# Decoder layer step on one Trainium2 core: layer norms with shifted, compact statistics, and the last norm finished on token rows

## The reference, cut to what matters

```
x = post(x, 0.5 * swiglu(mod(x, 0), ffn1), 0)        # FFN 1
m = mixer(mod(x, 1))                                 # attention over pages, and convolution
x = post(x, m, 1)
x = post(x, 0.5 * swiglu(mod(x, 2), ffn2), 2)        # FFN 2
mod(t, i)     = t * (1 + scale_i(c)) + shift_i(c)
post(t, y, i) = layernorm(alpha * t + gate_i(c) * y, ln_g[i], ln_b[i])
layernorm(v)  = (v - mean(v)) * rsqrt(mean((v - mean(v))^2) + 1e-5) * g + b    # over 1024 features
```

## Time and profile before

| | us |
|---|---|
| median of 3 runs (lowest, highest) | 938.13 (937.85, 939.4) |
| profiled execution, its own time | 937.36 |
| its span, first to last instruction | 935.5 |

### The profile page before, as it was taken

The page is one execution under the profiler, slowest core; times in us unless marked ns, Lnnn a source line. Parts: engine busy times, 40 slices in busy tenths (PEclk is TensorE's granted clock), DMA queues, the critical chain, the costliest instruction groups (busy, mean ns, idle before and its releaser), DMA issues.

```text
span 935.5 us, 16896 instructions
## 1 busy us (share of the span) xinstructions
PE 854.9 (91%) x6712; PEld 751.9 (80%) x6712; DVE 470.2 (50%) x751; ACT 343.2 (37%) x465; POOL 267.1 (29%) x319
## 2 busy tenths in 40 slices
PE   5699999998799988999986889869889999999997
PEld 3499989997699968988764556538789999999995
DVE  1543433432233379753686776743773454453436
ACT  2323332331222255454443324363363433432223
POOL 2020000000010013999999999600220000000000
PEclk9599999999799999999999999989999999999999
DMA  9957778777677442433998999996414544634301
GB/s 305 350 191 259 231 231 258 230 232 255 206 234 244 150 142 84 152 126 119 348 319 265 365 350 374 348 347 222 134 54 138 171 135 147 195 125 158 124 1 57
DMA packets 181521, 195.87 MB, mean 209 GB/s; under 512 B 11811, under 2 KB 163609, under 8 KB 181445
## 3 DMA queue, kind: packets, MB, share of 16 engines
q1 hardware_dynamic: 174541, 188.47, 61.9%
q10 hardware_dynamic: 6624, 6.33, 2.1%
q0 software_dynamic: 288, 0.14, 0.1%
HBM read 192.09 MB, written 3.17 MB: 209 GB/s over the span
## 4 chain that ended last, share of the span: by engine, by line
PE 78%; DVE 11%; DMA 5%; ACT 3%; issue 2%; SPq 1%; ACTq 0%; DVEq 0%
PE bank L1409 19%; PE bank L1410 18%; PE bank L1411 18%; PE bank L1625 5%; PE bank L1385 3%; PE bank L1650 3%; PE bank L1720 2%; DVE wlo L973 2%; PE bank L1374 1%; PE bank L1422 1%; DVE kT L1214 1%; PE bank L1423 1%; PE bank L1424 1%; DMA raw<-in_w_ada 1%; DMA xrow<-in_x_sample 1%
## 5 line engine op out<-in xcount | busy, mean ns | idle before, releaser
L973 DVE TENSOR_TENSOR wlo<-raw,whi 128x2048 fp32r<-128x2048 f32 (+1 forms) x80 | 190.8, 2386 | 257.6 <-ACT whi L656 256.3
L1409 PE MATMUL bank<-mh,whi 128*128 128x320 f32 x824 | 261.0, 317 | 4.5 <-DVE wlo L973 4.5
L1411 PE MATMUL bank<-mh,wlo 128*128 128x320 f32 x824 | 255.5, 310 | 0.0
L1410 PE MATMUL bank<-ml,whi 128*128 128x320 f32 x824 | 255.4, 310 | 0.0
L656 ACT CAST whi<-raw 128x2048 fp32r<-128x2048 f32 (+1 forms) x80 | 148.5, 1861 | 258.6 <-PE bank L1411 171.3
L1409 PEld LDWEIGHTS bank<-mh,whi 128*128 128x128 f32 x824 | 155.7, 189 | 15.3 <-issue 10.3
L1410 PEld LDWEIGHTS bank<-ml,whi 128*128 128x128 f32 x824 | 155.9, 189 | 0.0
L1411 PEld LDWEIGHTS bank<-mh,wlo 128*128 128x128 f32 x824 | 155.5, 189 | 0.0
L1409 PE MATMUL bank<-hh,whi 128*128 128x320 f32 x352 | 109.7, 312 | 0.0
L1410 PE MATMUL bank<-hl,whi 128*128 128x320 f32 x352 | 108.6, 309 | 0.0
L1411 PE MATMUL bank<-hh,wlo 128*128 128x320 f32 x352 | 108.6, 308 | 0.0
(11 more groups left out here) (237 smaller groups left out, 1151.8 us busy)
## 6 DMA issues: line engine op xcount, KB each, us to landing
...
```

Source lines behind the costliest of these rows:

```text
L973: dve.tensor_tensor(wl(slot_w(phase, u))[:, 0:size], landed(phase, u)[:, 0:size], wh(slot_w(phase, u))[:, 0:size].bitcast(F32), ALU.subtra ...
L1409: pe.matmul(bank[:, b, 0:T], wh(slot)[:, c], h_, start=(start and n == 0), stop=False)
L1410: pe.matmul(bank[:, b, 0:T], wh(slot)[:, c], l_, start=False, stop=False)
L1411: ins = pe.matmul(bank[:, b, 0:T], wl(slot)[:, c], h_, start=False, stop=(stop and n == len(parts) - 1))
```

## The change

- **Shift.** After the first four chunks of `yT` POOL has their sum (three additions). PE multiplies it by 1/1024 (`shift`, one matmul between two products: in DN1 and DN2 after the first half of unit 7, in WOUT after that of unit 2). DVE subtracts twice that, which is the mean of these 512 features, from the four chunks it has and from the last four chunks of `xT`, to which the later results are added (four instructions of 640 columns).
- **Statistics.** ACT squares chunk by chunk as they come, POOL adds the squares and chunks 4 and 5 (`square_sum`, `late_sum`), and PE takes mean and mean square of the shifted values with 64 output partitions for each half of the tokens (`spread`: two matmuls of 160 columns each). Difference, root and reciprocal are on 160 columns; two matmuls spread the result over 128 partitions again. A one-element root ahead loads ACT's table.
- **Scaling.** DVE subtracts the rest of the mean two chunks at a time, in the loop of chunks, and multiplies from PSUM.
- **alpha** is multiplied once into gain and bias of the first two norms; `scale_x` stays only for the first sub-layer.
- **Slots.** WIN's units 0 to 8 take slots 2, 0, 1 in turn, unit 9 slot 0. `lo(WIN, 1)` stands between the last two residuals, `hi(WIN, 2)` after the root. The first two units of w_out land in `kvw`, the last value pages take `araw`.
- **WOUT.** Four products of it move ahead in the last value pages; the first two banks are finished before the other two.
- **UP2.** Its first four banks are summed together, chunk by chunk.
- **Last norm.** PE sums each token's values with the activations as weights (`token_sums`: four matmuls with one column), transposes the shifted `yT`, and DVE finishes on token rows with mean and root per partition: two instructions of 512 columns for each of five pieces. Gain and bias come by DMA on all partitions. The two instructions on `xT` chunks in `norm` under `elif q % 2` are never reached, since `norm` now runs for n < 2 alone.

```diff
-        return phase[0] + u - (2 if u < 2 else 3)
+        if u == 0:
+            return -1
+        return phase[0] + u - (2 if u == WIN[2] - 1 else 3)
...
-        return (WIN[0] + 9, WIN[0] + 7, WIN[0] + 8, WOUT[0])[u]
+        return (WIN[0] + 9, WIN[0] + 8, WIN[0] + 6, WOUT[0])[u]
...
-                for q in range(1, NCH - 1):
+                for q in range(1, 4):
...
+            def late_sum(n):
+
+                pool.wait_ge(y_ready, 8 * n + 6)
+                pool.wait_ge(shift_ready, n + 1)
+                pool.tensor_tensor(tmp[:, 3, :], yT[:, 4, :], yT[:, 5, :], ALU.add).then_inc(ysum_step, 1)
...
+            def norm(n):
+
+                y_sums(n)
+                for q in range(1, 5):
+                    square_sum(n, q)
+                late_sum(n)
+                square_sum(n, 5)
...
+            pool.tensor_scalar(par1[:, 72:88], par1[:, 72:88], ALPHA, None, ALU.mult)
+            pool.tensor_scalar(par1[:, 96:112], par1[:, 96:112], ALPHA, None, ALU.mult).then_inc(fold_ready, 1)
+            norm(0)
...
-            scale_x(1)
...
+                    act.wait_ge(yc_ready, 2 * n + q // 2 + 1)
+                else:
+                    act.wait_ge(y_ready, 8 * n + q + 1)
+                if q >= 2:
+                    act.wait_ge(sqsum_step, 5 * n + max(q - 2, 1))
+                act.activation(tmp[:, q % 2, :], yT[:, q, :], ACT.Square).then_inc(sq_ready, 1)
...
+                    if u == 7:
+                        for q in range(4):
+                            square(n, q)
+                    if u == 9:
+                        square(n, 4)
+                        square(n, 5)
...
+            def norm(n, first, meanwhile=lambda: None):
+
+                act.wait_ge(ld_con, 16)
+                act.activation(warm[:, :], con[:, C_EPS:C_EPS + 1], ACT.Sqrt)
+                for q in range(first, NCH):
+                    square(n, q)
+                act.wait_ge(rest_ready, n + 1)
+                act.activation(tmp[:, 0, 0:NSPREAD], bank[:, NORM_BANKS[n][2], 0:NSPREAD], ACT.Square).then_inc(dsq_ready, 1)
+                act.wait_ge(vd_ready, n + 1)
+                act.activation(tmp[:, 0, 0:NSPREAD], tmp[:, 0, 0:NSPREAD], ACT.Sqrt, scale=16.0 ** -2, bias=con[:, C_EPSQ:C_EPSQ + 1]).then_inc(std_ready, 1)
+                meanwhile()
...
-            hi(WIN, 2)
-            norm(0)
+            down(DN1, WIN, 0)
+            norm(0, 6, lambda: hi(WIN, 2))
...
+            for q in range(4):
+                square(1, q)
             hi(UP2, 1)
-            norm(1)
+            norm(1, 4)
...
-                    dve.wait_ge(v_used, 24 + 5 + u)
...
+                dve.wait_ge(shift_ready, n + 1)
+                for q in (0, 1):
+                    y = yT[:, 2 * q:2 * q + 2, :]
+                    dve.scalar_tensor_tensor(y, sums, -2.0, y, ALU.mult, ALU.add).then_inc(yc_ready, 1)
+                for q in (2, 3):
+                    x = xT[:, 2 * q:2 * q + 2, :]
+                    dve.scalar_tensor_tensor(x, sums, -2.0, x, ALU.mult, ALU.add).then_inc(xs_ready, 1)
+                dve.wait_ge(xs_ready, 2 * n + 2)
...
+                    if u == 7:
+                        shift(sub)
...
+                            if nxt is not None and last and cc == 0:
+                                lo(nxt, u + SLOTS - phase[2])
...
+                dve.wait_ge(var_ready, n + 1)
+                dve.wait_ge(dsq_ready, n + 1)
+                dve.tensor_tensor(small[0], bank[:, NORM_BANKS[n][3], 0:NSPREAD], small[0], ALU.subtract).then_inc(vd_ready, 1)
+                dve.wait_ge(std_ready, n + 1)
+                dve.reciprocal(small[1], small[0]).then_inc(nr_ready, 1)
...
+                centre(0)
+                dve.wait_ge(spread_mm, 2 * n + 2)
...
+                    if q in (2, 4, 6):
+                        centre(q // 2)
+                    dve.wait_ge(yd_ready, 4 * n + q // 2 + 1)
+                    y = y.rearrange("p (g t) -> p g t", g=2)
+                    dve.tensor_tensor(y, y, scales, ALU.mult).then_inc(xn_ready, 1)
...
+            lo(WOUT, 2)
             for u in range(WOUT[2]):
-                if u < 2:
-                    lo(WOUT, u + 2)
-                elif u == 3:
+                if u == 2:
                     lo(UP2, 0)
+                    shift(1)
                 for cc in range(2):
                     n = 2 * u + cc
                     add_residual(1, n, bank[:, 2 * (u % 2) + cc, :], (n_ready, 4 + u + 1) if cc == 0 else (w_used, WOUT[0] + u + 1))
-            norm(1, lambda: lo(UP2, 1))
+                    if n == 1:
+                        lo(WOUT, 3)
+                    if n == 5:
+                        lo(UP2, 1)
+            norm(1)
             up(1, UP2, DN2)
...
+                if n == 0:
+                    dve.wait_ge(ld_rows, 16 * 6)
+                c = slice(512 * half, 512 * half + 512)
+                dve.scalar_tensor_tensor(yrow[:, tt, c], bank[:, OUT_BANKS[n], :], t_mean[:, tt:tt + 1], grow[:, c] if tt < 2 else grow_s,
+                                         ALU.subtract, ALU.mult).then_inc(centred, 1)
...
+                dve.scalar_tensor_tensor(yrow[:, tt, c], yrow[:, tt, c], t_inv[:, tt:tt + 1], brow[:, c] if tt < 2 else brow_s,
+                                         ALU.mult, ALU.add).then_inc(out_row, 1)
...
+            dve.wait_ge(rest_ready, 3)
+            link(dve.tensor_copy(t_mean, bank[:, 0:3, 0]))
+            link(dve.tensor_tensor(t_sq, t_mean, t_mean, ALU.mult))
+            dve.wait_ge(var_ready, 3)
+            dve.tensor_tensor(t_sq, bank[:, 3:6, 0], t_sq, ALU.subtract).then_inc(vd_ready, 1)
...
+            for n in range(5):
+                if n + 1 < 5:
+                    centre_rows(n + 1)
+                scale_rows(n)
...
+                        products([(2 * x + cc, slot_w(phase, x), cc, ((gr, ur)[x], w_used)[cc]) for x in range(2) for cc in range(2)],
                                  m_parts(range(NCH)), lambda n: pe.wait_ge(ml_ready, ml0 + n + 1))
-                        product(3, slot_w(phase, 1), 1, m_parts(range(NCH))).then_inc(w_used, 1)
...
+                pe.wait_ge(ysum_step, 4 * n + 3)
+                pe.matmul(bank[:, NORM_BANKS[n][0], 0:T], lnones, tmp[:, 3, :], start=True, stop=True).then_inc(shift_ready, 1)
...
+                    if u == 9:
+                        pe.wait_ge(yc_ready, 4 * ffn + 2)
...
+                        if u == 7 and cc == 0:
+                            shift(2 * ffn)
...
+                def spread(b, src, part):
+
+                    for g in range(2):
+                        ins = pe.matmul(bank[HG * g:HG * g + HG, b, 0:NSPREAD], lnones[:, 0:HG], src[:, NSPREAD * g:NSPREAD * g + NSPREAD],
+                                        start=part == 0, stop=part == 2)
+                    return ins
+
+                pe.wait_ge(y_ready, 8 * n + 7)
+                pe.wait_ge(ysum_step, 4 * n + 4)
+                spread(rest, tmp[:, 3, :], 0)
+                pe.wait_ge(sqsum_step, 5 * n + 5)
+                spread(sq, tmp[:, 2, :], 0)
+                spread(rest, yT[:, 6, :], 1)
+                pe.wait_ge(sq_ready, 8 * n + 7)
+                spread(sq, tmp[:, 0, :], 1)
                 pe.wait_ge(y_ready, 8 * n + 8)
-                pe.matmul(bank[:, 0, 0:T], lnones, yT[:, 7, :], start=False, stop=True).then_inc(mean_ready, 1)
-                keep_clock(2, 4)
-                for q in range(4):
-                    pe.wait_ge(sqsum_ready, 4 * n + q + 1)
-                    ins = pe.matmul(bank[:, 1, 0:T], lnones, squares(q)[:, 0, :], start=q == 0, stop=q == 3)
-                ins.then_inc(var_ready, 1)
-                keep_clock(0, 8)
+                spread(rest, yT[:, 7, :], 2).then_inc(rest_ready, 1)
+                pe.wait_ge(sq_ready, 8 * n + 8)
+                spread(sq, tmp[:, 1, :], 2).then_inc(var_ready, 1)
+                pe.matmul(bank[:, full, 0:T], lnones, tmp[:, 3, :], start=True, stop=False)
+                for q in (6, 7):
+                    ins = pe.matmul(bank[:, full, 0:T], lnones, yT[:, q, :], start=False, stop=q == 7)
+                ins.then_inc(mean_ready, 1)
+                pe.wait_ge(nr_ready, n + 1)
+                for g in range(2):
+                    pe.matmul(bank[:, out + 2 * g, 0:NSPREAD], lnones[HG * g:HG * g + HG, :], tmp[HG * g:HG * g + HG, 1, 0:NSPREAD],
+                              start=True, stop=True).then_inc(spread_mm, 1)
+                keep_clock(2, 5)
...
+            pair_values(3, {2: group_scales, 5: lambda: conv_half(0, 0, NCC), 6: lambda: conv_half(1, 0, 2)})
+            conv_half(1, 2, 3)
             attn_turn(3)
-            conv_half(1, 2, NCC)
-            products(first, m_parts(MIX_ORDER[NCC:]), lambda n: pe.wait_ge(ml_ready, 16 + NCC + n + 1), start=False)
+            conv_half(1, 3, NCC)
+            for u in range(2):
+                products(first[2 * u:2 * u + 2], m_parts(MIX_ORDER[NCC:]), lambda n: pe.wait_ge(ml_ready, 16 + NCC + n + 1), start=False)
...
```

(28 more changed lines are left out.)

178 lines of the change are left out of this document (102 added, 76 removed).

## The result

| kernel | median us | runs, lowest to highest | against the kernel before |
|---|---|---|---|
| before | 938.93 | 6, 937.85 to 941.01 | 1 |
| after | 929.12 | 6, 927.76 to 930.23 | 0.9894 (0.9880 to 0.9909) |

The change makes the kernel 9.8 us faster. I had forecast 14.9 us, and 929.12 lies 0.6 us above the upper end of my range. The sign and most mechanisms held. The size did not: two new waits of PE brought a lower clock with them that the sum had no term for, and the term of the value pages was too large.

What follows compares the result with a forecast made beforehand. Bound: a chain of PE stretches, where the distance from PE's last product before a norm to its first steady one behind counts. Terms: +1.1 (shifts in DN1, DN2) - 8.1 + 1.0 - 4.0 - 4.9 = -14.9, giving 923.2 us, range 918.5 to 928.5.

Steps and rivals of the forecast that it cites:

- the term of the value pages: Last value pages: 24 products of `conv_half(0)` move one page ahead into PE's idle time, -2.65 us (0 to -3.6).
- the collision with `scale_x`: WIN's third unit: `lo(WIN, 2)` took 7.92 us beside a POOL instruction; its removal ends PE's 2.99 us wait.
- the new collision in WOUT: WOUT: `lo(UP2, 0)` on DVE holds up POOL's third addition, 2.86 us instead of 0.87; PE waits 3.05 us.
- B: First norm to the start of WIN's third unit: 23.6 us instead of 31.7, so -8.1 us.
- D: Second norm to UP2's third unit: start at E+27.35, with PE waiting 3.9 us; -4.0 us.
- E: PE's end at a norm: the start of the last residual less 0.04 us; the forecast counts times from it.
- F: Last norm, from PE's end to the end of the span: 15.6 us instead of 20.5, so -4.9 us.
- rival 3: Middle bound by the stream of caches or POOL, so B's gain fills with waiting: 931.3 us; chance 0.07.
- Rival 4: Chunk loops at both norms: small PE waits bring 1.2 GHz, 23 us more, 946.2 us; chance 0.03.
- C: Value pages and WOUT: -2.65 for moved products, +3.05 wait, +0.56 matmul; +1.0 us, between -2 and +2.5.
- rival 2: Clock falls to 1.2 GHz after new idle stretches in WOUT and UP2, 1.5 us each: 924.7 or 926.2; chance 0.14.
- stretch 3: From the first product of WIN's third unit to PE's end at the second norm; forecast +1.0 us.

Runs made afterwards that it cites:

- wide_before: The kernel before with one more, unread column in the second load of the table of constants (1,835 instead of 1,834); 938.95 us, 0.9993.
- fill_before: The kernel before with 5, 3 and 3 unread fp32 matmuls where PE waits for the last value pages; 936.84 us, 0.9972.

## Why the prediction was wrong

**What held.** The order of things and most of the sizes: the reciprocal on half the columns, the end of the collision with `scale_x`, the new collision in WOUT (2.84 us where 2.86 was read from the earlier trace rows) and PE's wait of 2.78, the joint end of UP2's four banks and its wait of 3.76, the tail. B was forecast 0.6 and D 0.3 us too good: the first product starts at E+9.35 and E+8.9, and the two rows of products take 14.8 and 15.0 us, not 14.6. F was forecast 0.4 too poor. The middle moved as a piece, against rival 3: the ninth unit of WIN starts at 397.78 instead of 401.68, 3.9 us earlier, and a matmul on keys late in the middle (L1809, before L1650) at 590.07 instead of 594.08. Rival 4's half speed in the loops of chunks did not come: the clock is 1.00 there at both norms, in spite of the holes.

**What failed: the waits in C (3.05) and D (3.9) stand in the sum at their length alone, without a price for the clock.** I had looked at the idle time around the norms, and not at where the new idle time lies. The stall of 2.78 us in WOUT and the one of 3.76 us in UP2 each bring a fall to 1.2 GHz, of 1.4 and 1.5 us. It was in the text as rival 2 with 0.14, and the argument against it was one row behind a wait of 2.99 us, where the clock had not fallen. That row was no exception: `wide_before` waits 3.00 us in the same place, and its next stretch has clock 1.00 too (a row of its timeline, then one of its stretches).

```profile
367.72 0.41 PE L1409 MATMUL bank<-mh,whi 128*128 128x320 f32 x1 [3.00 <-DVE wlo L973]
...
368.00:372.00 4.00, 4.00 (x31) 4.00 (x31) 4.00 (x6) 0.45 (x2) 0.00 (x0) 1.00 0.84 262
```

But the clock fell behind all four waits of 3.76 us in UP2 and all four of 2.78 and 2.79 us in WOUT, and not behind the one of 2.58. So the length of a wait alone doesn't tell whether a fall follows; what else decides it is open. Rival 2 gave 926.2 for two falls; both came, and 929.12 was measured, most of the rest being the value pages.

"I assume that gone, since PE idles less" was said of the 1.5 us of half clock in the row of products behind the second norm. These did go: in the eight profiles of new programs no product there is slow. But as far as one profile shows, they cost the old program nothing either, for a wait behind them took them up. In `fill_before` that row runs at clock 1.00, PE then waits 2.08 us for `wlo` instead of 1.48, and the third unit starts 31.36 us after E, where the kernel before has 31.34.

**The term of the value pages was mis-sized.** -2.65 is more than the whole idle time of 2.30 us which it was to fill, and the prediction does not work it out. The edit also moves more than the 24 products named there: the 12 of `conv_half(1, 0, 2)` go one page ahead with them, and 6 more (not four, as the section on the change says) go ahead of the turning of the attention. On average the turning of the attention comes 0.7 us earlier after WIN than in three profiles of old programs (238.8 against 239.5). Behind it stand 0.9 us fewer of products, and there is a new wait of 0.4 us for DVE: -1.2 in all. Filling the idle time of the old order with unread matmuls brought 3.6 us in the same stretch. The unread matmuls need no page and do no work; what changed with them is the clock, which was 0.50 to 0.71 between 624 and 636 us and is 1.00 there now. So a large part of what idle time costs there is the clock it takes along, and moved products do not prevent that as long as they stand behind the first two waits.

**The account.** Without the start, and with stretch 3 taken from the ninth unit of WIN to E on average over four profiles of new programs with the collision (267.2 us) and three of old ones (263.2): +0.6 - 7.5 + 4.0 - 3.7 + 2.1 - 5.3 = -9.8, which is what the medians differ by. Against -14.9 that is 3.0 in C, 1.5 behind D, 0.6 in B and 0.3 in D, less 0.4 in F. The 3.0 in C are 1.4 of pages and 1.4 of clock, less 0.3 because the wait was 2.78 and not 3.05; some 0.4 us stay open. That the account meets the medians to the tenth is partly luck. The ratio's interval is 1.4 us to either side, stretch 3 differs by 2.4 us in the two profiles of the table and by 4.0 in these averages, and the start is left out, though the means of its four and eight profiles differ by 0.8 us.

**The start has no part in the miss.** The sum holds only differences, and 0.77 us were added to get from the profiled execution to the median. The +3.7 us in the first row of the table come from comparing two single profiles: the kernel before has one of the three early starts among four of old programs, the kernel after has the latest of eight. How far a start varies can't be seen in one profile; that it hung on a landing awaited for 9.72 us could be.

The Trainium skill (*TensorE: Matmul & The Clock Gate*, Part 1) says of a kernel's start that how many matmuls run at the low clock differs from run to run of the same kernel. These runs show the like later on: behind one and the same wait of 2.03 us in DN1 the clock fell in three of twelve profiles. So no single row, like that of the earlier trace rows, is evidence that a wait somewhere else is free.
